# Another order of the steps inside an attention cycle, in a transformer kernel on one core

## The chip, the core and the metric

One core of a Trainium2 chip runs the whole program. TensorE (PE) multiplies matrices, VectorE (DVE) and ScalarE (ACT) work on elements, GpSimd (POOL) does small things and loads rows, SyncE (SP) issues the weight loads. Each engine takes its own instructions in order and waits on semaphores for the others. The metric is device time in microseconds of one launch, the median of several runs.

## What is computed

Two small transformers over 256 tokens of width 1024, one behind the other: four layers whose mixers are sliding-window attention, a gated linear recurrence, latent attention and sliding-window attention again, each followed by a cross attention to a memory of 256 tokens and a gated feed-forward; then two layers whose mixers are a forgetting and a dilated attention, each with four heads that attend to the memory. All attentions have the same core:

```python
scores = jnp.einsum('bnqhgd,bnkhd->bhgqk', qb, kb) * scale     # masked with -1e30, or unmasked
probs = jax.nn.softmax(scores, axis=-1)                         # sliding: a sink joins the sum
out = jnp.einsum('bnhgqk,bnkhd->bnqhgd', probs, vb)
y = out.reshape(bsz, s, heads * head_dim) @ w_o
```

## The kernel before

One program walk (`program`) is executed once for each engine class (`Sync`, `Tensor`, `Scalar`, `Vector`, `Pool`); a method that an engine lacks is `nothing`. So the order of the calls in `attend` is the order of instructions on every engine at once, and what an engine does for one call is in its class.

Weights come in units of 128 x 1024 numbers (512 KB) through a ring of six buffers. ACT rounds each unit to `w_hi` (L1296), DVE makes the rest `w_lo` (L1706), and every projection is three products, `w_hi` with `x_hi`, `w_lo` with `x_hi`, `w_hi` with `x_lo` (L683 to L685). `Splitter.units` has both engines split the unit four ahead of the one that PE takes, at the place in the walk where PE takes one.

An attention runs over groups: two heads each (sliding 8 groups, latent 4, forgetting and dilated 6 and then 2 groups of memory heads), or one wide head (cross, 4 groups). For a group there are these steps:

- `scores` (PE; L809, L907, L970, L1053, L1205, L1245): into PSUM banks 2 and 3. A masked group's bank is free once DVE has masked it, an unmasked one's once ACT has taken its exponentials.
- `shift` (DVE; L1969, or L1959 and L1965, or L1974): masks the scores into one of two `e` buffers, row maxima, negated. It waits until the transposes of the group two before have read that `e` buffer.
- `exponentials` (ACT, L1535), with the row sums.
- `normalise` (DVE, L1998): `e` times the reciprocal of the sums.
- `transposes` (PE, L1026) into banks 4 and 5, and `probabilities` (ACT, L1547): their copy to `pt`.
- `values` (PE, L1040) into bank 6 or 7 by turns; free once `output` is through.
- `output`: ACT rounds the result to `xt_hi` (L1522), then DVE makes `xt_lo` (L1721).

`fill(e, c)` puts other work in a cycle: projections of later queries and keys in the first two or three cycles, later the `sum_unit`s of the output product, which need the finished outputs of two more tiles each. `settle` copies what the projections made. Behind `attend`, `out_finish` makes the second half of the output product, then comes the norm. In cycle c, the steps `shift` and `exponentials` are those of group c, `normalise`, `transposes` and `probabilities` those of group c-1, `scores` those of c+1, `values` those of c-2 and `output` those of c-3. The last group's `values` follow the filling work of cycle n+1.

PE therefore has, in a cycle: values, filling work, scores, transposes. ACT: output copy, splits, exponentials, copies of `settle`, probabilities. DVE: low part of the output, maxima, normalisation, splits (and rotations of queries and keys).

## Time and profile before

| | |
|---|---|
| median of 3 runs | 2281.13 us (2280.08 to 2281.62) |
| the profiled execution | 2280.59 us, span 2279.3 us |
| granted TensorE clock, mean | 0.967 |
| PE busy | 2113.0 us, 93% of the span |
| DVE busy | 1540.0 us, 68% |
| ACT busy | 1178.2 us, 52% |
| chain that ended last | PE 81%, DVE 10%, ACT 6%, issue 2% |
| idle time of PE before L1040 and L1026 | 21.3 us after ACT's `pt`, 11.5 us after DVE's `e` |

Busy time counts a matmul from its start to its modelled end, and the next one starts before that, so the time from one start to the next is what a matmul costs in a stream. An idle time in brackets stands ahead of the instruction it is shown with; behind it is the instruction that released it. A row of the timeline can stand for several instructions in a run (x8). The timeline's x counts an f32 matmul twice.

### The profile page before, as it was taken

The page shows a single profiled execution, that of the slowest core. Times are in us where ns is not written, and L with a number is a line of the kernel's source. Part 1 is how long each engine was busy: PE and PEld are TensorE (multiplying, and loading weights), DVE is VectorE, ACT ScalarE, POOL GpSimd, SP SyncE. Part 2 cuts the span into 40 slices and gives each one's busy share as a digit, 9 for nine tenths or more (in the row PEclk, how much of TensorE's full clock was granted, in tenths as well). Part 3 has the DMA queues.
Part 4 walks back from the last instruction along what each step waited for, and adds up shares of the span by engine and source line. Part 5 has one row for each costly group of instructions (what it writes and reads, how often), then busy time and mean ns, then how long its engine had stood idle before and what let it go on. Part 6 is the DMA issues. An engine that isn't in the chain of part 4 may idle for free.

```text
span 2279.3 us, 34081 instructions
## 1 busy us (share of the span) xinstructions
PE 2113.0 (93%) x13749; PEld 1916.5 (84%) x13749; DVE 1540.0 (68%) x2655; ACT 1178.2 (52%) x2027; POOL 92.2 (4%) x160
## 2 busy tenths in 40 slices
PE   7989999888999989999989899998988999999998
PEld 7858899787799978889977778997976999787997
DVE  4665777786677676577677657777455766656776
ACT  4444455493365545445545435554354555465554
POOL 3000000000000010000000000001000000000000
PEclk9999999998999999999999999998998999999999
DMA  8414666455366553466643337664524665434662
GB/s 278 145 56 141 182 183 181 137 167 175 109 197 183 172 155 121 130 177 184 194 153 120 117 106 213 191 180 135 156 75 130 194 194 183 152 95 121 194 186 92
DMA packets 436205, 356.24 MB, mean 156 GB/s; under 512 B 15858, under 2 KB 381686, under 8 KB 436048
## 3 DMA queue, kind: packets, MB, share of 16 engines
q1 hardware_dynamic: 429296, 332.49, 48.5%
q0 software_dynamic: 6752, 21.57, 2.8%
q8 instruction: 109, 1.79, 0.3%
q14 instruction: 48, 0.39, 0.1%
HBM read 352.97 MB, written 1.05 MB: 155 GB/s over the span
## 4 chain that ended last, share of the span: by engine, by line
PE 81%; DVE 10%; ACT 6%; issue 2%; POOL 1%; DMA 1%; SPq 0%; DVEq 0%; ACTq 0%
PE psum L683 20%; PE psum L685 20%; PE psum L684 20%; PE psum L1144 14%; PE psum L1040 3%; DVE w_lo L1706 1%; PE psum L970 1%; ACT e L1535 1%; DVE x_tok L2052 1%; ACT pt L1547 1%; DVE xt_lo L1721 1%; PE psum L1026 1%; DMA tok<-in_mem_dram 1%; DVE n_tok L2030 1%; ACT w_hi L1296 1%
## 5 line engine op out<-in xcount | busy, mean ns | idle before, releaser
L1706 DVE TENSOR_TENSOR w_lo<-w_raw,w_hi 128x1024 fp32r<-128x1024 f32 x639 | 751.9, 1223 | 144.2 <-ACT w_hi L1296 142.6
L683 PE MATMUL psum<-xt_hi,w_hi 128*128 128x256 f32 x2744 | 790.1, 288 | 26.9 <-DVE w_lo L1706 18.6
L684 PE MATMUL psum<-xt_lo,w_hi 128*128 128x256 f32 x2744 | 785.8, 286 | 0.0
L685 PE MATMUL psum<-xt_hi,w_lo 128*128 128x256 f32 x2744 | 785.8, 286 | 0.0
L1296 ACT CAST w_hi<-w_raw 128x1024 fp32r<-128x1024 f32 x639 | 646.8, 1049 | 80.3 <-PE psum L685 58.0
L683 PEld LDWEIGHTS psum<-xt_hi,w_hi 128*128 128x128 f32 x2744 | 537.0, 196 | 34.7 <-DVE w_lo L1706 11.8
L684 PEld LDWEIGHTS psum<-xt_lo,w_hi 128*128 128x128 f32 x2744 | 536.6, 196 | 4.7
L685 PEld LDWEIGHTS psum<-xt_hi,w_lo 128*128 128x128 f32 x2744 | 536.0, 195 | 0.0
L2121 DVE SCALAR_TENSOR_TENSOR qt<-psum,par,qt 128x255 f32<-128x255 f32 (+1 forms) x528 | 218.1, 476 | 163.9 <-ACT qt L1604 163.5
L683 PE MATMUL psum<-w_hi,xt_hi 128*128 128x512 f32 (+4 forms) x700 | 264.7, 378 | 14.8 <-DVE xt_lo L1721 13.7
L684 PE MATMUL psum<-w_lo,xt_hi 128*128 128x512 f32 (+4 forms) x700 | 256.1, 366 | 0.0
L685 PE MATMUL psum<-w_hi,xt_lo 128*128 128x512 f32 (+4 forms) x700 | 255.9, 366 | 0.0
L1604 ACT ACTIVATE qt<-psum,par 128x256 f32<-128x256 f32 x264 | 134.5, 560 | 212.2 <-PE psum L685 212.2
L1144 PE MATMUL psum<-w_hi,hid_hi 128*128 128x512 f32 x528 | 207.7, 393 | 4.8 <-DVE hid_lo L2133 4.8
L1144 PE MATMUL psum<-w_lo,hid_hi 128*128 128x512 f32 x528 | 207.0, 392 | 0.0
L1144 PE MATMUL psum<-w_hi,hid_lo 128*128 128x512 f32 x528 | 205.4, 389 | 0.0
L1721 DVE TENSOR_TENSOR xt_lo<-psum,xt_hi 128x512 fp32r<-128x512 f32 (+1 forms) x130 | 76.4, 620 | 149.3 <-ACT xt_hi L1522 121.2
L683 PEld LDWEIGHTS psum<-w_hi,xt_hi 128*128 128x128 f32 x700 | 138.0, 197 | 41.4 <-DVE w_lo L1706 9.0
L685 PEld LDWEIGHTS psum<-w_hi,xt_lo 128*128 128x128 f32 x700 | 137.6, 197 | 20.0
L684 PEld LDWEIGHTS psum<-w_lo,xt_hi 128*128 128x128 f32 x700 | 138.1, 197 | 18.0
L1609 ACT ACTIVATE kt<-qt 128x256 f32<-128x256 f32 x132 | 55.2, 418 | 181.2 <-DVE qt L2121 181.0
L1336 ACT CAST xt_hi<-psum 128x512 fp32r<-128x512 f32 x78 | 40.9, 591 | 185.3 <-PE psum L751 185.3
(216 smaller groups left out, 1920.6 us busy)
## 6 DMA issues: line engine op xcount, KB each, us to landing
w_raw<-in_f_w_up_dram SPq DMA_DIRECT2D x176, 512.0 KB, 5.0
w_raw<-in_f_w_down_dram SPq DMA_DIRECT2D x88, 512.0 KB, 5.1
w_raw<-in_w_up_dram SPq DMA_DIRECT2D x88, 512.0 KB, 4.7
w_raw<-in_w_down_dram SPq DMA_DIRECT2D x44, 512.0 KB, 5.1
w_raw<-in_x_w_q_dram SPq DMA_DIRECT2D x32, 512.0 KB, 4.2
w_raw<-in_x_w_o_dram SPq DMA_DIRECT2D x32, 512.0 KB, 4.7
w_raw<-in_a_w_qkv_dram SPq DMA_DIRECT2D x24, 512.0 KB, 4.5
w_raw<-in_w_in_fox_dram SPq DMA_DIRECT2D x20, 512.0 KB, 4.6
```

Of the source, the lines that this page charges most:

```text
L683: self.eng.matmul(out, stat[0], mov[0], start=first, stop=False)
L684: self.eng.matmul(out, stat[0], mov[1], start=False, stop=False)
L685: return self.eng.matmul(out, stat[1], mov[0], start=False, stop=last)
L1040: ins = self.eng.matmul(m.psum[p0:p0 + wide, k, slot * SEQ + q0:(slot + 1) * SEQ], vals(c), m.pt[:, group.g % 2, i, cols], start=c == 0, s ...
L1144: ins = self.eng.matmul(m.psum[:, b + 2 * c, :], stat[x], unit[y][:, 0, cs], start=False, stop=last and x == 1, skip_group_check=True)
L1296: self.up(self.eng.copy(self.m.hi[:, s, :], self.m.raw[:, s, :]), "w_hi", u)
L1336: self.up(self.eng.copy(dst[0][:, j:j + nt, :], self.m.pair(4 + j // 2)[:, 0:nt, :]), "x_hi", self.tag, after, j)
L1604: ins = self.eng.activation(m.qt[:, 2 * s + half, :], out[half], ACT.Identity, scale=col((TAPS - 1) * 2 * FT + half * FT + q), bias=col(TA ...
L1609: self.up(self.eng.activation(m.kt[:, s, :], m.qt[:, 2 * s + silu_half, :], ACT.Silu), "silu", self.tag, q)
L1706: self.up(self.eng.tensor_tensor(self.m.lo[:, s, :], self.m.raw[:, s, :], self.m.hi[:, s, :].bitcast(F32), ALU.subtract), "w_lo", u)
L1721: n = self.up(self.eng.tensor_tensor(dst, src, hi.bitcast(F32), ALU.subtract), "ready", (tag, what), j)
L2121: ins = self.eng.scalar_tensor_tensor(cv[:, d:SEQ], out[half][:, 0:SEQ - d], col((TAPS - 1 - d) * 2 * FT + half * FT + q), cv[:, d:SEQ], A ...
```

## The change

`attend` gets a parameter `lag` and walks the cycle in another order; the groups that a cycle works on stay the same, except that in the cross attention (`lag` 2) `output` is that of group c-2. PE now has: filling work, scores(c+1), values(c-2), transposes(c-1). ACT: filling work (splits), output copy, exponentials, settle, probabilities; in the cross attention the output copy comes behind the exponentials. DVE: maxima, normalisation, filling work, low part of the output. `fill_first` and `fill_last` put the filling work first on all engines but DVE, where it comes behind the normalisation. The loop has one cycle more, and the `sum_unit`s stand one cycle later (in the cross attention the first three stand in the same cycle as before, and the fourth half, `sum_unit(2, (0,))`, a cycle earlier). In the sliding attention the turning of the late queries moves from cycle 2 to cycle 3; in the dilated one `late_keys` and `memory_queries` go ahead of the turns.

```diff
@@ -284,6 +284,9 @@
     def nothing(self, *args):
         pass
 
+    def fill_first(self, fill, c):
+        fill(self, c)
+
 
     start = memory_keys_values = turn_params = first_features = second_memory = end = nothing
     norm_rows = norm_part = norm_part_last = add_part = norm_finish = norm_finish_last = norm_to_features = nothing
@@ -294,49 +297,65 @@
     keep_forgetting_tiles = dilated_start = late_queries = turn_late_queries = keep_late_queries = nothing
     late_keys = turn_late_keys = keep_late_keys = memory_queries = keep_memory_queries = nothing
     scores = shift = exponentials = normalise = transposes = probabilities = values = output = nothing
-    sum_unit = out_finish = feed_forward = nothing
-
-
-def attend(e, groups, fill, settle):
+    sum_unit = out_finish = feed_forward = fill_last = nothing
+
+
+def attend(e, groups, lag, fill, settle):
+
 
 
     n = len(groups)
     e.scores(groups[0])
-    for c in range(n + 3):
-        if c >= 3:
-            e.output(groups[c - 3])
-        if 2 <= c <= n:
-            e.values(groups[c - 2])
+    for c in range(n + 4):
+        e.fill_first(fill, c)
         if c < n:
             e.shift(groups[c])
         if 1 <= c <= n:
             e.normalise(groups[c - 1])
-        fill(e, c)
-        if c == n + 1:
-            e.values(groups[n - 1])
+        e.fill_last(fill, c)
+        if c + 1 < n:
+            e.scores(groups[c + 1])
+        if 2 <= c <= n + 1:
+            e.values(groups[c - 2])
+        if 1 <= c <= n:
+            e.transposes(groups[c - 1])
+        if lag == 3 and lag <= c < n + lag:
+            e.output(groups[c - lag])
         if c < n:
             e.exponentials(groups[c])
+        if lag == 2 and lag <= c < n + lag:
+            e.output(groups[c - lag])
         settle(e, c)
-        if c + 1 < n:
-            e.scores(groups[c + 1])
         if 1 <= c <= n:
-            e.transposes(groups[c - 1])
             e.probabilities(groups[c - 1])
 
 
 def narrow_sums(e, c):
 
-    if c in (4, 6):
-        e.sum_unit(c // 2 - 2)
-    elif c == 8:
+    if c in (5, 7):
+        e.sum_unit((c - 5) // 2)
+    elif c == 9:
         e.sum_unit(2, (0,))
-    elif c == 9:
+    elif c == 10:
         e.sum_unit(2, (1,))
-    elif c == 10:
+    elif c == 11:
         e.sum_unit(3)
 
 
 def wide_sums(e, c):
+
+    if c == 4:
+        e.sum_unit(0)
+    elif c == 5:
+        e.sum_unit(1, (0,))
+    elif c == 6:
+        e.sum_unit(1, (1,))
+        e.sum_unit(2)
+    elif c == 7:
+        e.sum_unit(3)
+
+
+def early_sums(e, c):
 
     if c == 3:
         e.sum_unit(0)
@@ -344,8 +363,9 @@
         e.sum_unit(1, (0,))
     elif c == 5:
         e.sum_unit(1, (1,))
+        e.sum_unit(2, (0,))
     elif c == 6:
-        e.sum_unit(2)
+        e.sum_unit(2, (1,))
         e.sum_unit(3)
 
 
@@ -353,16 +373,13 @@
     def fill(e, c):
         if c < 2:
             e.query_half(c)
-        elif c == 2:
+        elif c == 3:
             e.turn_query_half()
+            e.keep_query_half()
         narrow_sums(e, c)
 
-    def settle(e, c):
-        if c == 2:
-            e.keep_query_half()
-
     e.sliding_start(j)
-    attend(e, groups_of(SLIDING), fill, settle)
+    attend(e, groups_of(SLIDING), 3, fill, Engine.nothing)
 
 
 def latent(e):
@@ -378,14 +395,14 @@
             e.keep_latent_query(c + 2)
 
     e.latent_start()
-    attend(e, groups_of(LATENT), fill, settle)
+    attend(e, groups_of(LATENT), 3, fill, settle)
 
 
 def cross(e, l):
     def fill(e, c):
         if c < 2:
             e.cross_query(c + 2)
-        wide_sums(e, c)
+        early_sums(e, c)
 
     def settle(e, c):
         if c < 2:
@@ -395,7 +412,7 @@
     for j in range(2):
         e.cross_query(j)
         e.keep_cross_query(j)
-    attend(e, groups_of(CROSS), fill, settle)
+    attend(e, groups_of(CROSS), 2, fill, settle)
 
 
 def forgetting(e):
@@ -409,7 +426,7 @@
             e.keep_forgetting_tiles(c + 3)
 
     e.forgetting_start()
-    attend(e, groups_of(FORGETTING, MEMORY), fill, settle)
+    attend(e, groups_of(FORGETTING, MEMORY), 3, fill, settle)
 
 
 def dilated(e):
@@ -417,11 +434,11 @@
         if c == 0:
             e.late_queries()
         elif c == 1:
+            e.late_keys()
             e.turn_late_queries()
-            e.late_keys()
         elif c == 2:
+            e.memory_queries()
             e.turn_late_keys()
-            e.memory_queries()
         narrow_sums(e, c)
 
     def settle(e, c):
@@ -432,7 +449,7 @@
             e.keep_memory_queries()
 
     e.dilated_start()
-    attend(e, groups_of(DILATED, MEMORY), fill, settle)
+    attend(e, groups_of(DILATED, MEMORY), 3, fill, settle)
 
 
 def program(e):
@@ -1700,6 +1717,11 @@
 class Vector(Splitter):
 
 
+    fill_first = Engine.nothing
+
+    def fill_last(self, fill, c):
+        fill(self, c)
+
     def split(self, u):
         s = u % RING
         self.wait_ge("w_hi", u)
```

## Rows read from the trace of the kernel before

**Rows 1.** windows, first sliding, forgetting, dilated attention: us, busy of each engine (instructions)

```profile
core 0: us, PE busy (x) PEld busy (x) DVE busy (x) ACT busy (x) POOL busy (x), PEclk, DMA share, GB/s
109.35:152.56 43.21, 33.94 (x193) 24.59 (x191) 27.41 (x123) 23.80 (x82) 0.00 (x0) 0.96 0.16 47
...
1666.50:1717.40 50.90, 44.33 (x263) 33.98 (x260) 30.12 (x89) 26.00 (x79) 0.00 (x0) 0.97 0.18 54
2007.54:2062.76 55.22, 48.39 (x306) 39.42 (x305) 33.16 (x118) 29.08 (x90) 0.00 (x0) 0.97 0.23 70
```

**Rows 2.** who waited for whom, PE, whole span: total us, times, longest

```profile
PE psum L1040 <- ACT pt L1547: 21.3, 42, 1.4
```

**Rows 3.** timeline, first sliding, DVE and ACT: start, us, engine, line [idle before <-releaser]

```profile
117.76 0.42 DVE L1721 TENSOR_TENSOR xt_lo<-psum,xt_hi 128x256 fp32r<-128x256 f32 x1 [2.67 <-ACT xt_hi L1522]
118.10 0.28 DVE L1969 CUSTOM_DVE_ANT_0 e<-psum,mask 128x128 f32<-128x128 f32 x1
...
118.86 0.42 DVE L1969 CUSTOM_DVE_ANT_0 e<-psum,mask 128x256 f32<-128x256 f32 x1
...
120.21 1.01 DVE L1998 TENSOR_SCALAR e<-e,stat 128x128 f32<-128x128 f32 x4
...
121.78 0.83 ACT L1547 COPY pt<-psum 128x384 f32<-128x384 f32 x2
```

**Rows 4.** timeline, first sliding attention, PE, cycles 3 to 5

```profile
117.13 1.24 PE L1040 MATMUL psum<-pt,v 128*64 128x256 f32 x8 [1.43 <-ACT pt L1547]
118.88 1.55 PE L809 MATMUL psum<-kt,qt 128*128 128x128 f32 x8 [0.51 <-DVE stat L1969]
...
122.38 1.15 PE L1040 MATMUL psum<-pt,v 128*64 128x256 f32 x8 [0.57 <-ACT pt L1547]
...
126.33 1.47 PE L809 MATMUL psum<-kt,qt 128*128 128x128 f32 x8
127.64 0.82 PE L1026 MATMUL psum<-ident,e 128*128 128x128 f32 x6
128.70 1.25 PE L1040 MATMUL psum<-pt,v 128*64 128x256 f32 x8 [0.24 <-ACT pt L1547]
```

**Rows 5.** timeline, last cycles of the first sliding attention, PE without waits

```profile
149.62 0.82 PE L1026 MATMUL psum<-ident,e 128*128 128x128 f32 x6
150.19 0.48 PE L683 MATMUL psum<-w_hi,xt_hi 128*128 128x512 f32 x1
...
151.76 0.88 PE L1040 MATMUL psum<-pt,v 128*64 128x256 f32 x8
152.56 0.50 PE L683 MATMUL psum<-w_hi,xt_hi 128*128 128x512 f32 x1
```

**Rows 6.** timeline, first sliding attention, cycle 2, behind the rotation

```profile
111.97 0.29 DVE L1969 CUSTOM_DVE_ANT_0 e<-psum,mask 128x128 f32<-128x128 f32 x1
...
114.69 1.01 PE L1026 MATMUL psum<-ident,e 128*128 128x128 f32 x6 [0.30 <-DVE e L1998]
```

**Rows 7.** timeline, forgetting attention, DVE, cycle 3

```profile
1678.75 0.73 DVE L1959 SCALAR_TENSOR_TENSOR e<-psum,norm,mask 128x128 f32<-128x128 f32 x2
...
1680.82 0.61 DVE L1965 TENSOR_REDUCE stat<-e 128x1 f32<-128x128 f32 x2
```

**Rows 8.** timeline, dilated attention, cycle 6, DVE and PE

```profile
2044.28 1.28 DVE L1974 TENSOR_REDUCE stat<-psum 128x2 f32<-128x512 f32 x2
...
2047.78 1.99 PE L1053 MATMUL psum<-mem_kt,qrt 128*128 128x256 f32 x8 [0.26 <-ACT e L1535]
```

**Rows 9.** windows, first sliding attention; PEclk is the granted share of 2.4 GHz

```profile
140.28:143.97 3.69, 1.24 (x9) 0.82 (x9) 2.88 (x17) 1.50 (x6) 0.00 (x0) 1.00 0.47 138
145.71:149.12 3.41, 3.41 (x12) 2.28 (x11) 2.81 (x8) 1.27 (x3) 0.00 (x0) 0.50 0.03 7
```

**Rows 10.** timeline, first cross attention, PE and ACT

```profile
204.05 1.99 PE L1040 MATMUL psum<-pt,mem_v 128*128 128x256 f32 x8 [0.68 <-ACT pt L1547]
...
208.73 0.59 ACT L1522 CAST xt_hi<-psum 128x512 fp32r<-128x512 f32 x1
```

**Rows 11.** the page's first line

```profile
span 2279.3 us, 34081 instructions
```

## The prediction, made before the changed kernel was run

> **What bounds the kernel now.** The stage windows come first: TensorE (PE) is the engine that sets the end, and inside the attentions it is not full. In the stretch of the first sliding attention between its first transposes and its last `sum_unit` PE is busy 33.94 of 43.21 us; in the forgetting attention 44.33 of 50.90, in the dilated one 48.39 of 55.22 [rows 1]. The second sliding attention repeats the first to within 0.3 us. The list of waits says who is late there: PE's `values` wait for the probabilities of ScalarE (ACT), 21.3 us in 42 waits over the whole span [rows 2], and its `transposes` for the `e` that VectorE (DVE) normalises. Matmul durations overlap, so the wall time lost is larger than these waits: I go by starts.
>
> **The cycle as it is.** The timeline of one cycle without filling work shows the ring that sets its length. DVE takes the low part of an old output at 117.76, after 2.67 us of idleness ended by ACT's `xt_hi` copy; only then, at 118.10, do the masked maxima start; they end at 118.86 + 0.42 = 119.28; the normalisation runs 120.21 to 121.22; ACT copies the probabilities at 121.78 for 0.83, after its exponentials [rows 3]. PE: `values` at 117.13, scores at 118.88, next `values` at 122.38 [rows 4]. So the ring is: exponentials, probabilities, output copy, low part, maxima, exponentials; ACT and DVE take turns, and PE looks on. The period is 122.38 - 117.13 = 5.25 us, and 128.70 - 122.38 = 6.32 with a `sum_unit` in it. PE's own work at full speed is less: scores 127.64 - 126.33 = 1.31 [rows 4], transposes 150.19 - 149.62 = 0.57, values 152.56 - 151.76 = 0.80 [rows 5], together 2.68. A `sum_unit` is 12 products; six of them and the transposes between fill 150.19 to 151.76, so 6 cost about 1.4 and 12 about 2.75 (a little over 0.22 each, plus the start) [rows 5].
>
> **What the change does to the ring.** No instruction is added or removed: every term is a move. DVE starts a cycle with the maxima and does the low part last, so the low part no longer holds the maxima; ACT's output copy stands ahead of exponentials that have not been released yet. Their cover is the maxima and normalisation themselves, 1.8 and 1.3 us, against 0.4 us for the copy. The ring left runs mostly through PE, since the maxima of c+1 write the `e` buffer that `transposes(c-1)` reads: maxima of c 1.18 (119.28 - 118.10), hand-off 0.15 (the first head's maxima end some 0.15 before the scores start at 118.88), the second head's half of the scores 0.65, `values` 0.80, `transposes` 0.57 with a tail of 0.25 (its 0.82 at 127.64 against 0.57), hand-off 0.1. Sum: **3.8 us** a cycle instead of 5.25. DVE's own cycle is 1.8 + 1.3 + 0.4 = 3.5 and ACT's 0.4 + 1.9 + 0.8 = 3.1, just shorter. With a `sum_unit` PE is full: 2.75 + 2.68 = **5.4 us** instead of 6.32; DVE's 3.5 + 1.22 for one split hides in it.
>
> **Sliding attention, cycle by cycle.** Up to `transposes(0)` nothing moves. In cycle 2 DVE is still turning q1: the maxima start right behind it, at 111.97 [rows 6]. `scores(3)` waits for the maxima after that, and now `values(0)` and `turn_query_half` are queued behind it: PE idles from the end of `transposes(0)`, 109.6, to 112.7, a new stall of 3.1 us, where `values(0)` and the turn used to lie. But `transposes(1)` ends at 114.69 + 1.01 = 115.7 as before, being bound by the normalisation. Maxima start, new: cycle 3 at 115.8 (was 118.10), cycle 4 at 120.2 (the turn, 0.8, and its copies on ACT, 1.0, lie in between), 5 at 124.0, 6 at 129.4 (filled), 7 at 133.3. Cycle 7 has `sum_unit(1)` where there was nothing: 2.75 + 0.8 + 0.6 gives 136.9; in cycle 8 `values(6)` waits 0.6 for the probabilities and `transposes(7)` ends at 139.6. The sums are a cycle later, so the rest has no gap: half a sum 1.4, `values(7)` 0.8, half a sum 1.4, and the last `sum_unit` starts at **143.1**; before, 152.56 [rows 5]. Gain **9.4 us**, twice 18.8.
>
> **Forgetting.** Its maxima are longer: masking starts at 1678.75, the second head's reduce starts at 1680.82 and ends at 1681.43 [rows 7]. Cycles without filling work: second mask ready at 2.05, hand-off, half the scores (1.3), `values`, `transposes`: 5.15, where the same sum with DVE's ring gave about 6.2. In cycle 2 the tile products follow at once, worth 0.7 and, with the maxima freed, 1.9 by the start of cycle 3. Cycle 6 is the one that turns against the change: the memory scores have no mask, so `scores(7)` needs the bank that `exponentials(6)` frees. In the twin place of the dilated stage the maxima start at 2044.28 and `scores(7)` at 2047.78, 3.5 us later, with a `sum_unit` to cover it all but 0.26 [rows 8]. Now cycle 6 has no filling work: 3.5, then 1.83 for the scores (1.99 less the overlap), 0.8, 0.57, the tail and the hand-off make 7.0 us with 3.6 idle, hardly shorter than the filled cycle it replaces (about 7.4). The `sum_unit` moves to cycle 7, which was idle anyway. Adding up from cycle 3, the last `sum_unit` starts at 1710.2 instead of 1717.40: 7.2 us. **Dilated**: in cycle 1 `late_keys` now goes ahead of the turned queries and fills a wait for the rotation, worth some 1.4; the rotation of the late keys starts 2 us earlier, cycle 3 starts 3.5 earlier; two cycles without filling work at 3.7, one filled at 5.95, cycle 6 as above. Last `sum_unit` at 2055.4 instead of 2062.76: 7.3 us.
>
> **Clock.** After the 3.69 us in which PE was busy 1.24 us, the granted clock was 0.50, that is 1.2 GHz, from 145.71 to 149.12 [rows 9]: 3.41 us at half speed cost PE 1.7. The sum above takes the tail at full clock, so this stretch is gone from it; the new stalls (3.1 in cycle 2 of a sliding attention, 3.6 in cycle 6 of the two others) may each bring one. I charge 0.6 in each sliding attention (the one after its stall is partly under DVE's work) and 1.3 in each of the others. The Trainium skill, "TensorE: Matmul & The Clock Gate", section "HAM oscillation", says that pauses in TensorE's work throw it back to half rate and that it must warm up again each time; the row agrees for one stall. By that rule every new stall would cost the full 1.7, 6.8 instead of 3.8 in all, and the total would be 3 us worse.
>
> **Cross.** Four times, lag 2. Three waits of 0.68 for the probabilities go (`values` now stands behind `scores` or a sum) [rows 10]; each costs about 1.0 of wall time with the pipeline's drain, 3.0. New: `sum_unit(0)` and half of `sum_unit(1)` stand at the head of a cycle and need the output of the `values` just before them: ACT copy 0.59 [rows 10], low part about 0.7, hand-offs 0.3, less 0.36 of transposes: 1.2 to 1.5, twice. Net gain 0.5 each, 2.0 in all; bounds -1 (a third such wait) and +3 (none). **Latent.** Four groups; `scores(3)` stands ahead of `values(0)` and waits 1.0 for the maxima, and `sum_unit(0)` waits for the low part that is now behind the normalisation. No window row of its own; by the cross rows between 1.5 gained and 1.5 lost. I take 0.5 lost.
>
> **Sum.** 18.8 + 7.2 + 7.3 + 2.0 - 0.5 - 1.2 - 2.6 = 31.0 us. The profiled execution took 2280.6 (its span 2279.3 [rows 11] and 1.3 around it), the median is 2281.1, 0.5 above. 2281.1 - 31.0 = **2250**. The feed-forward and recurrent stages keep their order, and a stage that ends early moves the next one as a whole, since weights are loaded and split ahead of use.
>
> **Rivals.**
> *Half the gain* (0.14). My rings take each hand-off at its best. If a cycle takes 0.5 us more (DVE's 3.5 and ACT's 3.1 leave little room under 3.8), some 6 cycles in 4 stages give 12 back, and a second stall in the cross attentions 4: 2266. For it: every engine is now near the bound; against: the filled cycles are PE's alone.
> *More gain* (0.08). No new stall lowers the clock and the cross attentions lose their waits outright: 3.8 + 3 more, about 2243.
> *No change* (0.03). The splits of the output product's weights end late and PE waits for `w_lo` at `out_finish` for what it won: 2281. Against: they are asked for four units ahead, and 4 units take ACT 4.2 and DVE 4.9 of the 11 us of that product.
> *Slower* (0.05). One mechanism: the clock. `values` and `transposes` are now queued behind scores that wait for the maxima, so PE's idle time comes in one piece in every short cycle (1.1 us of 3.8) instead of three small ones. If that is enough to keep granting 1.2 GHz, each further 3.41 us costs 1.7, and the ring itself grows to 1.18 + 0.15 + 1.3 + 1.6 + 1.4 + 0.1 = 5.7, longer than today's 5.25. It decides from 31/1.7 = 18 further half-clock stretches, two for each of the nine attentions; with three each the time is 2281 + 46 - 31 = 2296. Against: today's short cycles idle half of 5.25 at full clock, and only the 2.4 us pause was followed by a fall.
>
> **How the numbers follow.** My forecast has 0.70, and its own spread, from the charged clock (3.8 less or 3 more), cross (3 either side) and latent (2), is 2243 to 2258. Half the gain reaches up to 2270. From 2242 to 2270 lies about 0.8. A measurement of this kernel can tell about 0.2% (4.6 us) from no change. Faster by more: 0.70 + 0.14 + 0.08 = 0.92; within: 0.03; slower: 0.05.
>
> **What the profile after should show.** In the waits, `values` on the probabilities well under 10 us, DVE's low part no longer waiting 1.7 to 2.7 for `xt_hi`; starts of the maxima in a sliding attention 3.8 and 5.4 apart; a PE idle of 3 us before `scores(3)` and of 3.6 before `scores(7)` of the two 8-group attentions with memory heads; two new waits of 1.2 to 1.5 on `xt_lo` in each cross attention; the last `sum_unit` of the first sliding attention at 143. Wrong would be: periods of 4.3 or more (then 2266), or a clock of 0.5 several times in an attention (then no gain).

## The result, and the profile after

The changed kernel took 2262.6 us in the median (2255.7 to 2263.1), the kernel before on the same chip 2280.6: a ratio of 0.9916, with a 95% interval from 0.9899 to 0.9933. The same program timed again beside the experiments gave 2258.5 (2257.0 to 2259.5), a ratio of 0.9898 (0.9881 to 0.9914). So the change saves about 18 to 23 us, where the forecast was 31; the forecast of 2250 is 8 to 13 us too low, and the time lies inside the forecast range. Single executions of this program lie 7 us apart and the fastest are those with the highest mean granted clock (2255.7 at 0.969, 2262.9 at 0.963). The second timing was to test that: it expected 2.3 us for each 0.001 of mean clock and got 0.6 (2257.0 at 0.968 to 2259.5 at 0.964), the first 1.2. So time and clock go together, but the clock's price came out at half or less of the expected one. That is why lengths are compared below together with their clock.

The profiled execution is the fastest of the first four, 2255.7, that is 24.9 less than the profiled one of before. Its page, the first line, and the shares of the chain that ended last:

```profile
span 2254.4 us, 34080 instructions
...
PE 83%; DVE 9%; ACT 4%; issue 1%; POOL 1%; DMA 1%; SPq 0%; DVEq 0%; ACTq 0%
```

The windows of the first sliding, the forgetting and the dilated attention, cut by the same marks as [rows 1] (length, busy time of PE, PEld, DVE, ACT, POOL with instructions, granted clock, DMA):

```profile
109.37:144.04 34.67, 29.49 (x194) 21.91 (x192) 27.66 (x125) 25.25 (x84) 0.00 (x0) 1.00 0.15 45
...
1652.50:1699.60 47.10, 41.37 (x261) 32.30 (x260) 30.46 (x90) 27.44 (x81) 0.00 (x0) 0.96 0.16 47
1986.87:2038.40 51.53, 46.09 (x306) 37.10 (x305) 33.48 (x120) 30.59 (x92) 0.00 (x0) 0.97 0.21 65
```

The work is the same; the stretches are 8.5, 3.8 and 3.7 us shorter. The first gained more than twice what the others did, though some 1.4 to 1.7 us of its 8.5 are a half-clock stretch of before ([rows 9]) that this execution doesn't have. By a half-clock stretch I mean 3.41 us at a granted clock of 0.50, as in that row; a stretch of twice the length is counted as two.

The waits of PE over the whole span (who waited for whom: us in total, times, the longest), then DVE's wait for ACT's output copy:

```profile
PE psum L826 <- DVE stat L1991: 9.1, 6, 3.1
PE psum L1070 <- ACT e L1552: 7.1, 2, 3.5
...
PE psum L1057 <- ACT pt L1564: 0.9, 3, 0.3
```

```profile
DVE xt_lo L1743 <- ACT xt_hi L1539: 39.2, 16, 2.9
```

`values` no longer waits for the probabilities: 0.9 us in 3 waits, where [rows 2] had 21.3 in 42. Two waits have grown from 0.5 us at most, and both were forecast: scores (L826) for the maxima, up to 3.1 us, and the memory scores (L1070) for `exponentials`, twice 3.5. The low part waits 2.9 us at most, and in 16 places only; in the kernel before the same pair of lines stands for 121.2 us in 52 waits.

The timeline of the first sliding attention shows the new cycle. DVE (start, us, line, [idle before <- what ended it]):

```profile
115.91 0.29 DVE L1991 CUSTOM_DVE_ANT_0 e<-psum,mask 128x128 f32<-128x128 f32 x1 [0.80 <-PE psum L1043]
...
120.28 0.29 DVE L1991 CUSTOM_DVE_ANT_0 e<-psum,mask 128x128 f32<-128x128 f32 x1 [0.91 <-PE psum L1043]
...
123.33 0.42 DVE L1743 TENSOR_TENSOR xt_lo<-psum,xt_hi 128x256 fp32r<-128x256 f32 x1
124.21 0.29 DVE L1991 CUSTOM_DVE_ANT_0 e<-psum,mask 128x128 f32<-128x128 f32 x1 [0.47 <-PE psum L1043]
...
129.87 0.29 DVE L1991 CUSTOM_DVE_ANT_0 e<-psum,mask 128x128 f32<-128x128 f32 x1 [1.06 <-PE psum L1043]
...
133.79 0.29 DVE L1991 CUSTOM_DVE_ANT_0 e<-psum,mask 128x128 f32<-128x128 f32 x1 [0.47 <-PE psum L1043]
```

and PE:

```profile
112.68 1.58 PE L826 MATMUL psum<-kt,qt 128*128 128x128 f32 x8 [3.06 <-DVE stat L1991]
114.19 0.88 PE L1057 MATMUL psum<-pt,v 128*64 128x256 f32 x8
...
120.98 1.58 PE L826 MATMUL psum<-kt,qt 128*128 128x128 f32 x8 [0.74 <-DVE stat L1991]
122.49 0.88 PE L1057 MATMUL psum<-pt,v 128*64 128x256 f32 x8
123.30 0.87 PE L1043 MATMUL psum<-ident,e 128*128 128x128 f32 x6
...
144.04 0.39 PE L700 MATMUL psum<-w_hi,xt_hi 128*128 128x512 f32 x1
```

The maxima (L1991) start at 115.91, 120.28, 124.21, 129.87 and 133.79; forecast were 115.8, 120.2, 124.0, 129.4 and 133.3. A cycle without filling work takes 3.9 us (3.8 forecast, 5.25 before), one with a `sum_unit` 5.7 (5.4 forecast, 6.32 before). The low part at 123.33 has no wait in front of it, where [rows 3] had 2.67; it is the maxima that wait now, 0.47 us, for PE's transposes: the ring runs through PE, as derived. In PE's rows scores, `values` and `transposes` follow one another without a gap, after one wait of 0.74 for the maxima. The last `sum_unit` starts at 144.04 (143.1 forecast, 152.56 in [rows 5]).

### The profile page after: what moved, and what is told of

Its sections match the earlier page's. It is cut to its first block, busy times and chain, and to the rows that moved or that the text cites. A ratio compares the mean times of both kernels' runs of the same rounds, so it can differ in the third digit from the quotient of the medians.

```text
span 2254.4 us, 34080 instructions
## 1 busy us (share of the span) xinstructions
PE 2100.3 (93%) x13749; PEld 1909.1 (85%) x13749; DVE 1539.6 (68%) x2655; ACT 1178.4 (52%) x2027; POOL 91.9 (4%) x160
## 3 DMA queue, kind: packets, MB, share of 16 engines
HBM read 352.97 MB, written 1.05 MB: 157 GB/s over the span
## 4 chain that ended last, share of the span: by engine, by line
PE 83%; DVE 9%; ACT 4%; issue 1%; POOL 1%; DMA 1%; SPq 0%; DVEq 0%; ACTq 0%
PE psum L700 20%; PE psum L702 20%; PE psum L701 20%; PE psum L1161 14%; PE psum L1057 3%; DVE w_lo L1728 1%; PE psum L1043 1%; PE psum L987 1%; DVE xt_lo L1743 1%; DVE x_tok L2074 1%; PE psum L826 1%; DMA tok<-in_mem_dram 1%; ACT w_hi L1313 1%; DVE n_tok L2052 1%; DVE small L2055 1%
## 5 line engine op out<-in xcount | busy, mean ns | idle before, releaser
L700 PE MATMUL psum<-w_hi,xt_hi 128*128 128x512 f32 (+4 forms) x700 | 261.8, 374 | 23.8 <-DVE xt_lo L1743 22.5
```

The lines of the kernel that those rows point to most:

```text
L700: self.eng.matmul(out, stat[0], mov[0], start=first, stop=False)
```

## Where the 24.9 us of the profiled pair lie

Each attention is measured here from its first scores to the last product before the norm, in us, with the time that TensorE lost in half-clock stretches in brackets (a stretch of 3.41 us at 1.2 GHz counts 1.71, and what a stage loses by it comes out as somewhat less, see below):

| stage | before | after | gain |
|---|---|---|---|
| first sliding | 72.6 (1.7) | 63.6 (0) | 9.0 |
| second sliding | 72.6 (1.7) | 66.3 (3.4) | 6.3 |
| forgetting | 85.9 (1.7) | 81.7 (1.7) | 4.2 |
| dilated | 78.6 (1.7) | 74.4 (1.7) | 4.2 |
| four cross | 52.7 each | 52.9 each | -0.75 in all |
| latent | 52.4 | 52.8 | -0.4 |

These make 22.5. The other 2.4 lie in the stretches between, mainly in half-clock stretches of stages whose order the change leaves alone, behind the forgetting attention above all; I don't count them as a gain of the change.

## The experiments

**e1_low_first.** VectorE's part undone alone: it takes the low part ahead of the maxima again, in the lag 3 attentions; ScalarE and TensorE stay as changed.

```diff
 class Vector:
+    output_early = True
 def attend(e, groups, lag, fill, settle):
     for c in range(n + 4):
+        if e.output_early and lag == 3 and lag <= c < n + lag:
+            e.output(groups[c - lag])
         e.fill_first(fill, c)
         ...
-        if lag == 3 and lag <= c < n + lag:
+        if not e.output_early and lag == 3 and lag <= c < n + lag:
             e.output(groups[c - lag])
```

> The changed kernel with VectorE alone back in its old place for one step: in the sliding, latent, forgetting and dilated attentions it takes the low part of the output at the head of the cycle, before the maxima. Theory A (the ring over ScalarE's output copy and VectorE's low part set the cycle, and taking the low part out of it is the gain): the maxima wait for xt_hi again by 1.7 to 2.7 us a cycle, the short cycles go back from 3.9 to about 5.2 us, the filled ones to 6.3 or more, since ScalarE now splits ahead of the copy; 2278 to 2285 us. Theory B (TensorE's new order is the gain: filling work and scores cover the probabilities that values used to wait for): VectorE's place matters little, 2256 to 2266 us.

Measured: 2292.8 us (2288.7 to 2300.7), ratio to the kernel before 1.0054 (1.0037 to 1.0072). The whole gain is gone, and some 12 us more. The timeline of its first sliding attention, DVE and ACT:

```profile
123.20 0.28 DVE L1995 CUSTOM_DVE_ANT_0 e<-psum,mask 128x128 f32<-128x128 f32 x1
...
129.10 1.06 ACT L1316 CAST w_hi<-w_raw 128x1024 fp32r<-128x1024 f32 x1
130.05 0.39 ACT L1542 CAST xt_hi<-psum 128x256 fp32r<-128x256 f32 x1
130.47 0.42 DVE L1747 TENSOR_TENSOR xt_lo<-psum,xt_hi 128x256 fp32r<-128x256 f32 x1 [4.15 <-ACT xt_hi L1542]
130.81 0.28 DVE L1995 CUSTOM_DVE_ANT_0 e<-psum,mask 128x128 f32<-128x128 f32 x1
```

The low part stands directly ahead of the maxima and waits 4.15 us for ACT's copy. In the changed order ACT takes a split of the weights (1.06 us) and then the copy, so that split now stands in the ring too. This cycle takes 130.81 - 123.20 = 7.6 us, but part of it is clock, as the windows show: the half-clock stretch in it, the cycle itself, and the other cycle with such a split, which ran at full clock.

```profile
124.70:128.11 3.41, 3.41 (x16) 2.06 (x15) 1.51 (x8) 1.96 (x9) 0.00 (x0) 0.50 0.00 0
123.20:130.81 7.61, 6.93 (x33) 5.09 (x34) 3.29 (x20) 4.04 (x13) 0.00 (x0) 0.78 0.00 0
135.97:142.07 6.10, 5.41 (x33) 4.29 (x34) 3.27 (x19) 3.91 (x13) 0.00 (x0) 1.00 0.30 89
```

So the cycle with the split in its ring is one of 6.1 us, against 5.2 for one without, and the other 1.5 are the clock. The loss beyond theory A has two parts. One is the split, which I had not thought of: against e9, below, which differs from e1 by ACT's order alone and whose profile has as many half-clock stretches in the attentions, it costs 8 us. The other is the clock: in the profiled execution the attentions have ten half-clock stretches, in that of the kernel before four. The six more are about 8 us at 1.4 each. PE now pauses for 1.9 to 2.1 us in several cycles.

**e2_dve_alone.** The reverse: the kernel before, with VectorE's low part last in the cycle of the sliding, forgetting and dilated attentions, and the sums one cycle later, as in the changed kernel. ScalarE and TensorE keep the old order of their steps. The run has this walk in a function of its own, `attend_late`; it is set here against `attend` of the kernel before, and the moved sums are left out.

```diff
 class Vector:
+    low_last = True
 def attend(e, groups, fill, settle):    # in the run: attend_late
-    for c in range(n + 3):
-        if c >= 3:
+    for c in range(n + 4):
+        if not e.low_last and 3 <= c < n + 3:
             e.output(groups[c - 3])
         ...
         if c == n + 1:
             e.values(groups[n - 1])
+        if e.low_last and 3 <= c < n + 3:
+            e.output(groups[c - 3])
```

> The kernel before with one part of the change in the sliding, forgetting and dilated attentions: VectorE takes the low part last in the cycle, and the sums stand one cycle later, since they need it. TensorE's and ScalarE's order, cross and latent attention are the old ones. Theory A: short cycles of about 3.9 us, filled ones about 5.9 (values wait 0.25 for the probabilities at the head and are not covered), and the stall of 3.1 us in cycle 2 of the sliding attention has values(0) and the turn in it: about 2260 to 2268 us, most of the gain. Theory B: short cycles stay at 5.2 us, 2277 to 2283 us.

Measured: 2259.4 us (2259.2 to 2260.7), ratio 0.9905 (0.989 to 0.992), the same as the whole change within the interval. DVE in its first sliding attention:

```profile
120.44 0.29 DVE L2001 CUSTOM_DVE_ANT_0 e<-psum,mask 128x128 f32<-128x128 f32 x1 [1.39 <-PE psum L1057]
...
123.48 0.42 DVE L1753 TENSOR_TENSOR xt_lo<-psum,xt_hi 128x256 fp32r<-128x256 f32 x1
124.20 0.29 DVE L2001 CUSTOM_DVE_ANT_0 e<-psum,mask 128x128 f32<-128x128 f32 x1 [0.31 <-PE psum L1057]
...
130.83 0.29 DVE L2001 CUSTOM_DVE_ANT_0 e<-psum,mask 128x128 f32<-128x128 f32 x1 [2.03 <-PE psum L1057]
```

The short cycle is 124.20 - 120.44 = 3.8 us, as with the whole change; the filled one is 6.6 against 5.7, so what e2 lacks is worth 1 us in each filled cycle (with TensorE's old order alone, in e3 below, it is 6.4). The sliding attentions take 65.5 us each and the dilated one 75.0, with no half-clock stretch, the forgetting one 82.1 with one. That makes three stretches fewer than in the profile of the kernel before, about 4 us. At equal clock VectorE's step is thus worth some 17 us in the attentions, three quarters of the 22.5 of the whole change; the changed kernel gains more by its order and has three stretches more. The later place of the sums isn't the cause, since e1 and e9 have it too. One row of the list of waits says what TensorE's order is for, and how little that wait weighs:

```profile
PE psum L1071 <- ACT pt L1578: 20.6, 42, 1.4
```

All 42 waits of `values` for the probabilities are still there, 20.6 us of them ([rows 2] had 21.3), and about 22 us of the time are gone. A wait that shows for an engine isn't what its removal is worth: that wait was where PE stood while the ring on the other two engines turned.

**e9_pe_alone.** The changed kernel with the output step first in the cycle on VectorE and ScalarE both: the new order remains on TensorE alone (in the cross attentions, as in e1, on all engines).

```diff
 class Vector:
+    output_early = True
 class Scalar:
+    output_early = True
```

> The changed kernel with both VectorE and ScalarE taking the output first in the cycle, as before, in all attentions but the cross ones; so only TensorE's order and the place of the sums are new. With VectorE alone put back the time was 2292.8 us, 12 above the kernel before; the trace of that run shows ScalarE's split of 1.05 us in front of the copy that VectorE then waits for, and filled cycles of 7.6 us. If that is its cause, this one has filled cycles of about 6.5 and short ones of 5.2, and takes 2280 to 2286 us: TensorE's new order alone wins nothing. If TensorE's order has a worth of its own without VectorE's, 2275 or less.

Measured: 2284.5 us (2280.5 to 2288.4), ratio 1.0021 (1.001 to 1.0032). The waits of its DVE, and of its PE for the probabilities:

```profile
DVE xt_lo L1748 <- ACT xt_hi L1543: 117.3, 47, 8.2
```

```profile
PE psum L1060 <- ACT pt L1568: 2.6, 5, 0.6
```

The mirror image of e2: the wait of `values` is gone, 2.6 us instead of 21.3, and the time is 4 us longer, since DVE's wait for the copy is at 117.3 (121.2 before). The cycle itself says more. The maxima of its first sliding attention, ahead of and behind a `sum_unit`, at full clock:

```profile
130.21 0.28 DVE L1996 CUSTOM_DVE_ANT_0 e<-psum,mask 128x128 f32<-128x128 f32 x1
...
135.84 0.28 DVE L1996 CUSTOM_DVE_ANT_0 e<-psum,mask 128x128 f32<-128x128 f32 x1
```

The filled cycle takes 5.63 us, as in the changed kernel, and not the 6.5 that were expected; the short ones take 5.15, as in the kernel before. So TensorE's order shortens the filled cycles by itself, and the short ones are the ring's. The clock took that gain away: each sliding attention takes 71.2 us with two half-clock stretches, where the kernel before takes 72.6 with one, and the attentions have ten stretches in all against four. At 1.4 us for each of the six more, the attentions would be 2 to 4 us shorter than before at equal clock (an estimate). In the measured time TensorE's order alone won nothing.

**e4_act_early.** ScalarE's output copy first in the cycle again, alone.

```diff
 class Scalar:
+    output_early = True
```

> The changed kernel with ScalarE alone back in its old place for one step: in all attentions but the cross ones it copies the output at the head of the cycle, ahead of the split of a weight unit. Theory A: VectorE needs the copy only behind its normalisation, so its place doesn't matter; 2256 to 2262 us, and the short cycles stay at 3.9 us. Rival (ScalarE's order, splits first, carries part of the gain): filled cycles grow by up to the 0.4 us of the copy, 8 of them, 3 us more.

Measured: 2256.5 us (2253.9 to 2261.2), ratio 0.9889 (0.9871 to 0.9907): no difference from the changed kernel. Once the low part comes last on DVE, it doesn't matter where ACT makes the copy. Between e1 and e9 the same edit of ACT is worth 8 us (2292.8 against 2284.5), and the clock isn't the reason: both profiles have ten half-clock stretches in the attentions, whose lengths differ by 8.7 us in all. ScalarE's new place costs only if the maxima wait behind the low part.

**e3_values_first.** The changed kernel with TensorE's steps in their old order, save in the cross attentions.

```diff
+        old = lag == 3
+        if old and 2 <= c <= n:
+            e.values(groups[c - 2])
         ...
         e.fill_last(fill, c)
+        if old and c == n + 1:
+            e.values(groups[n - 1])
         if c + 1 < n:
             e.scores(groups[c + 1])
-        if 2 <= c <= n + 1:
+        if not old and 2 <= c <= n + 1:
             e.values(groups[c - 2])
```

> The changed kernel with TensorE alone back in its old order in all attentions but the cross ones: values at the head of the cycle, then filling work, scores, transposes. Theory A: the ring through VectorE (maxima 1.8, normalisation 1.3, transposes 0.6 behind it) still gives 3.8 us for a short cycle, filled ones grow from 5.6 to about 5.9, and the stalls before scores(3) and scores(7) have values in them, which gives 0.8 back each; within 4 us of the changed kernel either way. Theory B: the gain is lost, 2272 us or more.

Measured: 2259.2 us (2258.2 to 2260.5), ratio 0.9903 (0.9889 to 0.9918). Its sliding attentions take 66.1 us both, without half-clock stretches. In the changed kernel the first takes 63.6 at full clock and the second, with two half-clock stretches, 66.3. TensorE's order is thus worth 2.5 us a sliding attention at full clock, and the clock took that back in one of the two. The wait in cycle 2 is what differs ahead of those two stretches; PE of e3's first sliding attention:

```profile
113.99 1.58 PE L831 MATMUL psum<-kt,qt 128*128 128x128 f32 x8 [1.58 <-DVE stat L1996]
```

1.58 us of idleness here, 3.06 in the changed kernel: `values(0)` stands ahead of the scores and cuts the pause (the turn comes in cycle 3 in both). That the shorter pause is why the clock stayed up is the reading, not shown by this run alone.

**e5_sums_6_7.** In the forgetting and the dilated attention the first two sums stand in cycles 6 and 7 instead of 5 and 7, so that cycle 6 has work for the wait of the memory scores.

```diff
+def memory_sums(e, c):
+    if c == 6:
+        e.sum_unit(0)
+    elif c == 7:
+        e.sum_unit(1)
+    elif c > 7:
+        narrow_sums(e, c)
```

> The changed kernel with the first sum_unit of the forgetting and dilated attentions in cycle 6 instead of 5, so that it lies in front of scores(7), which wait for the exponentials of group 6. My theory of the shortfall there (D: the bank that only the exponentials free leaves TensorE idle for 3.55 us, and the clock falls behind it): cycle 5 becomes a short one of about 3.9 (dilated) and 5.4 (forgetting), the idle time before scores(7) falls to about 0.9, and the half-clock stretch that follows it goes; 2.7 us less in each of the two attentions, 4.4 where the stretch goes too, so 5 to 9 us under the changed kernel: 2250 to 2254 us. Rival E (cycle 6 is bound by VectorE and ScalarE anyway, the sum only lengthens it): cycle 6 grows by what cycle 5 loses, no gain, 2257 to 2262.

Measured: 2251.0 us (2248.6 to 2254.5), ratio 0.9872 (0.9857 to 0.9887). The row of the changed kernel and its counterpart, PE in cycle 6 of the dilated attention:

```profile
2021.86 3.22 PE L1070 MATMUL psum<-mem_kt,qrt 128*128 128x256 f32 x8 [3.55 <-ACT e L1552]
```

```profile
2016.37 1.99 PE L1080 MATMUL psum<-mem_kt,qrt 128*128 128x256 f32 x8 [0.91 <-ACT e L1562]
```

The wait falls from 3.55 to 0.91 us, and the eight matmuls behind it take 1.99 instead of 3.22: behind the long wait they ran in part at 1.2 GHz (a stretch from 2022.47). The forgetting attention takes 79.2 instead of 81.7, the dilated one 71.3 instead of 74.4, neither with a half-clock stretch. That is 5.7 us, of which the two half-clock stretches that are gone account for about 3 and the filled wait for the rest. The profile of e7, below, separates the two: it has the same wait in the forgetting attention and no half-clock stretch (the wait, then the stage's window):

```profile
1684.27 1.99 PE L1110 MATMUL psum<-mem_kt,qrt 128*128 128x256 f32 x8 [3.55 <-ACT e L1592]
```

```profile
1633.57:1713.68 80.11, 74.29 (x471) 62.47 (x472) 49.48 (x127) 41.04 (x116) 0.79 (x2) 1.00 0.26 80
```

That is 80.1 us: 1.6 of the 2.5 that the forgetting attention gains in e5 are clock, 0.9 the filled wait.

**e6_half_rotation.** In the sliding attentions DVE rotates only one block of q1 ahead of the maxima of cycle 2, and the other behind them: half the delay that TensorE waits for there.

```diff
 class Vector:
     def query_half(self, c):
-            self.rotated_tokens("q1", (0, 1), BANK, 0)
+            self.rotate_block("q1", (0, 1), BANK, 0, 0)
 def sliding(e, j):
     def fill(e, c):
         if c < 2:
             e.query_half(c)
+        elif c == 2:
+            e.rotate_rest()
         elif c == 3:
```

> The changed kernel with the rotation of the late queries in the sliding attention cut in two on VectorE: the first token block stays in cycle 1, the second goes behind the normalisation of cycle 2. Theory: the maxima of group 2 start 2.1 us earlier, the idle time of TensorE before scores(3) falls from 3.07 to about 1.0, and cycle 3 starts 0.8 earlier, as VectorE has the same work; so 0.8 for each sliding attention from the ring, and up to 1.7 more where a half-clock stretch follows the stall today: 2 to 5 us in all, 2254 to 2259. Rival: the second half now holds up the maxima of cycle 3 and nothing is won, 2257 to 2262.

Measured: 2251.6 us (2250.6 to 2254.9), ratio 0.9876 (0.9861 to 0.9891). PE, the scores of cycle 2, and then the windows of both sliding attentions, of this kernel:

```profile
110.51 1.58 PE L828 MATMUL psum<-kt,qt 128*128 128x128 f32 x8 [0.95 <-DVE stat L2004]
```

```profile
93.75:156.70 62.95, 58.66 (x327) 46.19 (x328) 48.65 (x173) 35.54 (x109) 1.34 (x2) 1.00 0.31 96
1206.51:1269.46 62.95, 58.67 (x328) 46.16 (x329) 48.56 (x173) 36.82 (x110) 1.35 (x2) 1.00 0.31 95
```

and the same two of the changed kernel:

```profile
93.83:157.41 63.58, 58.40 (x327) 46.21 (x328) 48.74 (x173) 35.53 (x109) 1.34 (x2) 1.00 0.31 94
1209.28:1275.58 66.30, 61.18 (x327) 48.12 (x328) 48.66 (x173) 37.16 (x110) 1.34 (x2) 0.95 0.30 91
```

The wait falls from 3.06 to 0.95. As long as the clock is 1.00 that is worth only 63.58 - 62.95 = 0.6 us, because the rotation's other half comes due a little later; but the second sliding attention, which lost 2.7 us to the clock, no longer does. These two make 4.0 us. The medians differ by 7 (2251.6 against 2258.5), more than the 2 to 5 that were expected. Of the 7, 1.3 are the ring. The five programs whose profile has the stall of 3.06 us and is otherwise that of the changed kernel there (the changed kernel, its second timing, e4, e5, e7) have 0 and 2, 1 and 1, 0 and 2, 0 and 1, 2 and 2 half-clock stretches in their two sliding attentions: 2.2 a program, about 3 us. That makes 4.4 of 7. The rest stays open; a profile shows one execution, and the one of e6 is its slowest.

**e7_cross_latent_old.** The cross and the latent attentions with the old order on all engines.

```diff
-    attend(e, groups_of(LATENT), 3, fill, settle)
+    attend_before(e, groups_of(LATENT), fill, settle)
-    attend(e, groups_of(CROSS), 2, fill, settle)
+    attend_before(e, groups_of(CROSS), fill, settle)
```

> The changed kernel with cross and latent attention walking as in the kernel before, sums included. By the stage lengths of the two profiles, the new order costs 0.2 us in each cross attention and 0.4 in the latent one, so this gives back 1.2 us: 2256 to 2261, hardly to be told from the changed kernel in time, but to be seen in the stage lengths (52.71 instead of 52.89 from the first scores to the last product of a cross attention). If the new order did help cross attention and the loss came from elsewhere (my forecast had 0.5 gained in each), these stages get longer.

Measured: 2256.8 us (2252.4 to 2261.8), ratio 0.9898 (0.9875 to 0.992): its time can't be told from the changed kernel's. The stage lengths can, since these stages repeat to 0.05 us: each cross attention goes back from 52.9 to 52.7, the latent one from 52.8 to 52.4. So the change loses 1.2 us in these five stages. Of the changed kernel, PE in the first cross attention:

```profile
200.09 0.47 PE L700 MATMUL psum<-w_hi,xt_hi 128*128 128x512 f32 x1 [1.05 <-DVE xt_lo L1743]
...
206.32 0.47 PE L700 MATMUL psum<-w_hi,xt_hi 128*128 128x512 f32 x1 [1.05 <-DVE xt_lo L1743]
```

These are the two new waits on `xt_lo`, 1.05 each.

**e8_all.** e5, e6 and e7 together.

> The three edits together (sums in 6 and 7 with memory heads, the rotation in two halves, cross and latent as before). If the causes are separate, the gains add: 5 to 9, 2 to 5 and 1.2 us under the changed kernel, 2245 to 2252 us. If the clock makes them overlap, less: down to 2254.

Measured: 2245.8 us (2244.6 to 2247.1), ratio 0.9848 (0.9834 to 0.9863). The dilated attention takes 71.2 us, the forgetting one 79.2, the sliding ones 62.9, none of them with a half-clock stretch, and the four executions lie 2.5 us apart.

**e10_halves.** e8 with the first two sums in halves, one half to a cycle: sliding cycles 5 to 8, and the second memory sum in cycles 7 and 8.

```diff
 def narrow_sums(e, c):
-    if c in (5, 7):
-        e.sum_unit((c - 5) // 2)
+    if c in (5, 6, 7, 8):
+        e.sum_unit((c - 5) // 2, ((c - 5) % 2,))
 def memory_sums(e, c):
     if c == 6:
         e.sum_unit(0)
-    elif c == 7:
-        e.sum_unit(1)
-    elif c > 7:
+    elif c >= 7:
         narrow_sums(e, c)
```

> The three edits of the version that took 2245.8 us, and the first sums cut in halves: in the sliding attention one half in each of the cycles 5 to 8 instead of whole ones in 5 and 7, in the attentions with memory heads the second one in halves in 7 and 8. In a short cycle TensorE has 2.8 us of work for 3.9, in a filled one 5.5 for 5.6; with a half in each, 4.2 for about 4.2. The idle 1.1 us of cycle 6 and 0.6 of cycle 8 go: 1 to 1.7 us in each sliding attention, up to 0.3 in the others, 2242 to 2245 us. If VectorE's splits of weights (1.2 us) and its 3.5 us of attention work then set the cycle, nothing is won, 2245 to 2247.

Measured: 2243.1 us (2241.2 to 2243.4), ratio 0.9832 (0.9817 to 0.9848). The sliding attentions take 62.0 us, 0.9 less than in e8, and the other two 0.5 less each: half a sum fills the gap that a short cycle leaves. It is the fastest version found, 15 to 20 us faster than the changed kernel.

## Why the prediction was right, and where it was off

**What bounds the kernel: right.** The ring from ACT's copy over DVE's low part to the maxima set the length of a short cycle. e2 shows it alone: one step moved on one engine gives the time of the whole change, 0.9905 against 0.9898 and 0.9916, and some 17 of 22.5 us at equal clock. e3 and e9 show the other side: TensorE's order is worth 2.5 to 3 us in a sliding attention at full clock, mainly in the filled cycles, and in both versions with long pauses (the changed kernel, e9) the half clock took much of it back, in e9 all of it. The prediction told the two apart less sharply than it should have; it opened with the 21.3 us of `values` [rows 2], and the time that wait stands for in the list is not what its removal won.

**The sliding cycle: right.** 3.9 and 5.7 us for 3.8 and 5.4, the new stall 3.06 for 3.1, the start of the last `sum_unit` 144.0 for 143.1, a gain of 8.5 up to there (9.0 over the whole stage) for 9.4. The terms of the short cycle add up to 3.7 and not to the 3.8 written behind them, so the sum was 0.2 short of the 3.9 measured: the scores take 122.49 - 120.98 = 1.51 us up to the start of `values`, where I had taken 1.31 from the kernel before, in which `transposes` follow them [rows 4]. In a filled cycle the difference is 5.66 against 2.75 + 2.68 = 5.43: scores 0.1 longer, sum and transposes about 0.07 each. PE of the filled cycle:

```profile
126.75 1.47 PE L826 MATMUL psum<-kt,qt 128*128 128x128 f32 x8
128.15 0.88 PE L1057 MATMUL psum<-pt,v 128*64 128x256 f32 x8
```

**Forgetting and dilated: the mechanism right, the size off.** Forecast were gains of 7.2 and 7.3 ahead of the clock's charge; measured are 4.2 each, with as much half-clock time before as after. The long wait of cycle 6 came as told, 3.55 us for 3.6. What was mis-sized are the terms around it. In the forgetting attention the maxima start at 1662.77, 1668.17, 1673.57, 1679.67 and 1688.40 in the changed kernel: periods of 5.40 where the sum had 5.15, and 6.10 for 5.95. From cycle 6 to 7 it takes 8.73 us, where the sum had 7.0 and a charge of 1.3. From the maxima of cycle 7 to the last `sum_unit` it takes 11.2 us, where the sum had 10.2. These are 0.25 + 0.25 + 0.15 + 0.4 + 1.0 = 2.05 us too little for the forgetting one, all on the same side: at every hand-off between engines I took the shortest that the rows showed. The forecast net of the clock was 5.9, measured 4.2: that is the difference, to 0.4. The dilated one repeats it: cycles of 3.99 and 3.92 us for 3.7, 6.08 for 5.95, 8.79 for 8.3, and 11.3 for the tail.

**The clock: the charge too small, and wrong in its nature.** I charged 0.6 for each sliding attention and 1.3 for each of the two others, 3.8 in all. The profiled execution has two stretches in the second sliding attention, 2.7 us, and one in each of the two others, about 3: some 5.7. The same program in the same stage took 63.6 us with no half-clock stretch, 65.0 with one (both sliding attentions of the second timing's profile: 64.9 and 65.2), and 66.3 with two. So one stretch costs about 1.4 (1.6 in the forgetting attention, e7 against the changed kernel), and whether it comes is not set by the program alone. In the second sliding attention of the changed kernel, the window of PE's stall, and the first of the two half-clock stretches, which begins inside it:

```profile
1225.08:1228.14 3.06, 0.00 (x0) 0.00 (x0) 2.96 (x10) 0.57 (x2) 0.00 (x0) 0.84 0.51 148
1227.16:1230.57 3.41, 2.43 (x8) 2.03 (x8) 3.20 (x18) 1.29 (x7) 0.00 (x0) 0.50 0.00 1
```

PE did nothing for 3.06 us, and the granted clock fell to 0.50 (1.2 GHz) before it began again. In the first sliding attention the same stall of the same length was followed by a clock of 1.00 to the end of the stage. The Trainium skill, "TensorE: Matmul & The Clock Gate", section "HAM oscillation", tells of a kernel whose TensorE waits some 3 to 5 us for transfers at each tile and starts every tile at half rate. Carried over to this kernel, as the prediction did, every new stall would cost; the 3.06 us here are at the lower end of those waits, and the traces show some that did and some that didn't. The stall of 3.55 us is no different: it was followed by a stretch in the changed kernel, by none in e7's forgetting attention. Shorter pauses are followed by one too: 2.0 us in the forgetting and the dilated attention of the kernel before, which the prediction's "only the 2.4 us pause" passes over, and 1.9 to 2.1 in e1 and e9, again not every time. What holds in all traces here is the other direction: where the longest pause had been cut to 1.3 us or less (e6, e8, e10 in the sliding attentions, e5, e8, e10 in the other two) not one half-clock stretch fell into these stages, and with 1.4 to 1.6 us (the sliding attentions of e2 and e3) none either. The rival "slower", in which PE's 1 us gap in each short cycle would keep the clock down, didn't come about: a gap of 0.74 in each short cycle went with a clock of 1.00. Its mechanism does show at more than twice that length: e1 and e9 have pauses of 1.9 to 2.1 us in several cycles, and five of e1's ten stretches begin right behind such a pause.

**Cross and latent.** Forecast were 2.0 gained and 0.5 lost; measured 0.75 lost and 0.4 lost. The latent term came out right, but by luck rather than by a sum: it had no row behind it and was put between 1.5 gained and 1.5 lost. In the cross attentions the new waits were sized well (1.05 us idle, 1.3 with the drain, for 1.2 to 1.5). What failed is the balance against the credit. The row ahead of the second wait, of the same stage:

```profile
204.66 0.60 PE L1043 MATMUL psum<-ident,e 128*128 128x128 f32 x4
```

From these transposes to the sum it takes 206.32 - 204.66 = 1.66 us. Transposes with no wait behind them take 0.36 to the sum (209.86 - 209.50 in the same stage), so a new wait costs 1.3; by the same count one of the three old ones, 0.68 in the rows [rows 10], cost 0.9, where I had booked 1.0. That is 2.6 against 2.7 us, next to no gain, and the stage came out 0.2 longer; that last bit I haven't traced. The lower bound of the term, -1, holds it (-0.75).

**The sum.** Against the forecast of 31.0 the profiled pair has 22.5 in the attentions: sliding 17.6 forecast with the clock's charge and 15.3 measured, forgetting 5.9 and 4.2, dilated 6.0 and 4.2, cross 2.0 and -0.75, latent -0.5 and -0.4. Those are 2.3 + 1.7 + 1.8 + 2.75 - 0.1 = 8.5 us: 3.5 of too short hand-offs, 2.75 of the cross attentions, 2.3 of the sliding attentions, which is the second one's clock. The medians are lower still, 18 and 23, because the profiled execution was the changed kernel's fastest. The time lies between the forecast and "half the gain" (2266), whose reason, rings that take each hand-off at its best, is what was found; it was priced at 0.5 us a cycle where the rows show 0.1 to 0.4.

**What stays open.** Why the same stall lowers the clock in one execution or stage and not in the other isn't settled: no experiment moved a stall in time without changing its length. Nor are some 2.6 of e6's 7 us accounted for.

## What to carry to other kernels

When three engines take turns, write the ring of hand-offs with their times from the timeline, and look first for a step that is ahead of the ring's work on its engine without belonging to it: here one low part of 0.4 us on VectorE held up everything, while removing 19 us of TensorE's waits at another line won no time alone (e9): the filled cycles got shorter, and longer pauses elsewhere brought the half clock. Then fill each new stall that the re-ordering creates, if only to one third of its length: beyond its own time it brings the half clock with it in some executions. And when adding up a ring from the rows, take the mean hand-off and drain, not the best: five such terms made 2 us of 7. Before one version is called worth more than another, count the half-clock stretches in both profiles.

## What the runs showed of the hardware

A pause of TensorE of 3.06 us was followed in one stage by two half-clock stretches of 3.41 us each, costing 2.7 of 63.6 us, and in the twin stage by none; in the stages where the longest pause had been cut to 1.3 us or less there was none. Complete pauses of 1.9 to 2.1 us were followed by a stretch in some places (before, e1, e9) and by none in others (e2's dilated attention). The cost of such a stretch to the stage was 1.4 to 1.6 us rather than the 1.7 that TensorE itself loses; that part of it lies under the other engines' work is my reading. The order in which ScalarE made a 0.4 us copy was worth 8 us or nothing, depending on VectorE's order alone (e1 against e9, e4 against the changed kernel), without a single instruction more or less.
